# A two-block transformer kernel: the second block's projections, in another order on ScalarE and VectorE, and the compressed scores in another order on TensorE

## The chip, the cores and the metric

The kernel runs on one core of a Trainium2 chip. The metric is the device time of one execution in microseconds. A core has TensorE (PE, matmuls; PEld in the profile is its weight loads), VectorE (DVE), ScalarE (ACT), GpSimd (POOL) and SyncE (SP, here the engine that issues the weights' transfers). They run side by side, each in its own program order, and wait for each other through semaphores.

## The reference

One sequence of 256 rows, width 1024, in float32, goes through two blocks. The first is a recurrent mixer with cross attention and a mixture of experts. The second, which the change touches, begins with one projection of the normalised rows that is cut into twelve parts, and a sparse attention over three kinds of keys, one of them compressed blocks of 32 rows:

```python
xn = rmsnorm(x, norm_mix)
(u_rnn, u_gate, q, k_c, v_c, k_s, v_s, k_w, v_w, g_nsa, g_a, g_b) = jnp.split(xn @ w_in, cuts, axis=-1)
...
qh = rmsnorm(q.reshape(B, T, N_HEADS, hd), q_norm) * (hd ** -0.5)
kc = rmsnorm(compress_blocks(kv(k_c), phi_k_pe, phi_k_w1, phi_k_w2), kc_norm)
...
# compress_blocks: 15 overlapping blocks of 32 rows, each with pe added, flattened, then
#   gelu(flat @ w1) @ w2
s_c = einsum("bgrqd,bgcd->bgrqc", qb, kc) + bias          # 16 heads, 256 rows, 15 blocks
p_c = masked_softmax(s_c, cend[None, :] <= tq[:, None])
```

x there is the first block's output after its own final norm; heads have 64 elements, 16 query heads share 4 groups of keys.

## The kernel before

Every product of a projection is done three times, as high x high, high x low and low x high halves of float32 values (lines 433 to 435, `mm3`), so each weight unit has to be split before TensorE can use it. The weights come as units of 128 x 2048 values (1 MB; those of ug 128 x 1792) in a fixed plan: kcvc 0 and 1, ksvs 0 and 1, kwvw 0 and 1, q2a 0 and 1, q2b 0 and 1, ug 0 and 1, w1 0 to 3, ug 2 to 5, then the units of the attention loop. A unit passes four stations:

- SP issues its transfer into one of four slots of a ring, when TensorE has used the unit that lay there, four places earlier (line 2563).
- ACT copies it to one of three buffers for high halves (`high`, L1175). It waits for the landing, and until TensorE has used the unit three places earlier.
- DVE writes the low half over the slot (`low`, L1731).
- TensorE waits for that (s_w_lo), multiplies, and sets the unit free (s_w_used).

On ACT and DVE both steps are written by hand between their other work as `ahead(key)`, which stands for the unit two places behind key. So `ahead(("ksvs", 0))` prepares kwvw 0, and `ahead(("ug", 0))` prepares w1 0. Nothing else sets the order: it is the order in the code.

In the second block's projections TensorE does the transposes of rows (turn 4 and turn 5, L443, and the row of scales, L453), kcvc, ksvs, the bias row (L883), kwvw, q2a, q2b, the gates (gn), ug 0 and 1, w1 0 to 3, ug 2, small transposes and products (L918 to L932), the queries' and keys' transposes (L951 and L958 among them), ug 3 and 4, the compressed scores (L973), ug 5, and the attention loop, whose scores are L999 and L1002. A unit of ksvs, kwvw or q2 is 24 matmuls of 512 columns; one of w1 is 24 of 256 columns with 60-column weights, one of ug 48 of 256 columns.

DVE and ACT do around this: `blocks(p)` (L2208, 16 small additions that build the overlapping blocks), whose result ACT copies to its high half (`block_high`, L1439) and DVE completes (L1740 with 960 elements); turn 5, that is `normalise(5)` on DVE (L1760, L1740) with `turn_high(5)` on ACT (L1193); four products of the residual rows with their scale (L2222); the bias row (L2229); reading out the projections' banks (L1463, L1464, L1467 on ACT); and the norms of the heads: squares on ACT (L1475), sums on DVE (L2232), the root on ACT (L1477), the products on DVE (L2238 and L2240, for each of the two row tiles).

The compressed scores are 64 matmuls with a weight of 64 rows (one head's elements) by 128 (rows of the sequence) and 15 columns. Even heads lie on partitions 0 to 63, odd heads on 64 to 127, and `head(h)` gives which. Each of the two kinds goes into a bank of its own.

## Time and profile before

| | us |
|---|---|
| median of 3 runs | 1296.73 (1295.91 to 1301.46) |
| the profiled execution | 1296.88 |
| its span | 1295.1 |
| PE, PEld busy | 1224.7 (95%), 1085.5 (84%) |
| DVE, ACT, POOL busy | 909.2 (70%), 722.9 (56%), 116.8 (9%) |
| mean granted clock of TensorE | 0.975 |
| second block's projections | about 728 to 866 in the span |

The 1.8 us beside the span lie before the first and after the last instruction that is recorded. Busy shares are means over stages with different limits, so the stage of the change has to be read by itself, by windows and by the timelines of its engines. A matmul's recorded duration is longer than its distance to the next, because they overlap; the distance is what it costs.

### The profile page before, as it was taken

To read this page: it belongs to the slowest core of one execution; us is meant where nothing else is said; L and a number is where in the kernel's file an instruction comes from. 1 tells how busy PE (TensorE), PEld (TensorE's weight loads), DVE (VectorE), ACT (ScalarE), POOL (GpSimd) and SP (SyncE) were. 2 spreads that over 40 slices of the span, in tenths; PEclk is the share of its full clock that TensorE was granted. 3 is DMA by queue.
4 is the path that set the end of the run, shared out by engine and by line. 5 is a ranking of instruction groups with operands and counts; after the bars stand their busy time and mean duration, and the time that the engine had idled before them with its cause. 6 is when DMAs were issued, how large, how long until landed. Compare 5 with 4: busy or idle time off the path is not lost. (4 is left out here: it accounts for less than half of the span.)

```text
span 1295.1 us, 18840 instructions
## 1 busy us (share of the span) xinstructions
PE 1224.7 (95%) x7850; PEld 1085.5 (84%) x7850; DVE 909.2 (70%) x967; ACT 722.9 (56%) x838; POOL 116.8 (9%) x135
## 2 busy tenths in 40 slices
PE   6999998988999999999998889999989999899998
PEld 6988996977888787887876868898989998799997
DVE  5997587447778888788888864558755975655553
ACT  4744324444577676766766345558768734444442
POOL 0100000000000000000000100009721520000000
PEclk8999999989999999999999889889999999899999
DMA  6433325315489888888987236422225446355552
GB/s 260 162 130 131 131 98 183 131 65 195 178 324 366 317 329 325 322 340 308 365 322 283 74 131 222 172 90 98 95 82 167 153 135 212 114 195 195 195 195 98
DMA packets 38179, 255.43 MB, mean 197 GB/s; under 512 B 4192, under 2 KB 6368, under 8 KB 10320
## 3 DMA queue, kind: packets, MB, share of 16 engines
q1 hardware_dynamic: 34800, 247.64, 53.2%
q10 hardware_dynamic: 3296, 6.61, 1.4%
q8 instruction: 62, 1.02, 0.3%
q14 instruction: 21, 0.17, 0.0%
HBM read 253.15 MB, written 1.08 MB: 196 GB/s over the span
## 5 line engine op out<-in xcount | busy, mean ns | idle before, releaser
L433 PE MATMUL bank<-r,r 128*128 128x512 f32 (+5 forms) x2016 | 672.3, 333 | 44.1 <-DVE r L1731 22.1
L1731 DVE TENSOR_TENSOR r<-f,r 128x2048 fp32r<-128x2048 f32 (+3 forms) x240 | 542.8, 2267 | 202.1 <-ACT r L1175 201.9
L435 PE MATMUL bank<-r,r 128*128 128x512 f32 (+5 forms) x2016 | 661.6, 328 | 0.0
L434 PE MATMUL bank<-r,r 128*128 128x512 f32 (+5 forms) x2016 | 661.3, 328 | 0.0
L1175 ACT ACTIVATE r<-f 128x2048 fp32r<-128x2048 f32 (+3 forms) x240 | 453.6, 1891 | 185.3 <-PE bank L435 168.6
L433 PEld LDWEIGHTS bank<-r,r 128*128 128x128 f32 (+4 forms) x2016 | 379.2, 188 | 90.5 <-issue 36.3
L434 PEld LDWEIGHTS bank<-r,r 128*128 128x128 f32 (+4 forms) x2016 | 379.5, 188 | 35.2 <-issue 1.0
L435 PEld LDWEIGHTS bank<-r,r 128*128 128x128 f32 (+4 forms) x2016 | 379.5, 188 | 34.8
L1740 DVE TENSOR_TENSOR r<-f,r 128x512 fp32r<-128x512 f32 (+3 forms) x70 | 54.9, 788 | 32.1 <-ACT r L1698 11.2
L2506 POOL TENSOR_SCALAR f<-f,f 128x128 f32<-128x128 f32 (+1 forms) x64 | 64.2, 1023 | 47.1 <-DVE f L2301 47.1
L443 PE MATMUL bank<-f,f 128*128 128x128 f32 x224 | 33.2, 310 | 9.0 <-DMA f<-in_cst 6.2
L443 PEld LDWEIGHTS bank<-f,f 128*128 128x128 f32 x224 | 31.5, 222 | 11.0 <-DMA f<-in_cst 6.2
L2470 POOL TENSOR_SCALAR f<-f 128x1 f32<-128x1 f32 x2 | 0.6, 292 | 416.4 <-ACT f L1186 416.4
L1193 ACT ACTIVATE r<-f 128x512 fp32r<-128x512 f32 x28 | 17.4, 631 | 30.3 <-DVE f L1760 30.3
L1696 ACT ACTIVATE f<-bank 128x512 f32<-128x512 f32 x16 | 9.6, 600 | 41.4 <-PE bank L435 41.4
L2457 POOL TENSOR_SCALAR f<-f 128x1 f32<-128x1 f32 x10 | 4.8, 480 | 307.1 <-ACT f L1186 306.9
L1186 ACT ACTIVATE f<-f 128x512 f32<-128x512 f32 x28 | 17.5, 625 | 22.1 <-DVE f L1802 9.8
L1747 DVE TENSOR_TENSOR f<-bank,f 128x512 f32<-128x512 f32 x28 | 18.7, 687 | 15.7 <-PE bank L443 15.6
L1564 ACT ACTIVATE f<-f,f 128x128 f32<-128x128 f32 (+1 forms) x64 | 28.3, 446 | 1.9 <-DVE f L2338 1.9
L1200 ACT ACTIVATE f<-bank 128x512 f32<-128x512 f32 x12 | 7.1, 593 | 27.4 <-PE bank L435 27.3
L2423 DVE TENSOR_TENSOR f<-f 128x512 f32<-128x512 f32 x16 | 11.1, 692 | 14.7 <-ACT f L1696 14.7
L1760 DVE TENSOR_TENSOR f<-f,bank 128x512 f32<-128x512 f32 x28 | 18.5, 682 | 3.2 <-PE bank L453 3.2
(314 smaller groups left out, 998.3 us busy)
## 6 DMA issues: line engine op xcount, KB each, us to landing
f<-in_weights SPq DMA_DIRECT2D x216, 1024.0 KB, 4.9
f<-in_weights SPq DMA_DIRECT2D x12, 896.0 KB, 4.7
f<-in_weights SPq DMA_DIRECT2D x8, 672.0 KB, 4.7
f<-in_weights SPq DMA_DIRECT2D x4, 882.0 KB, 5.3
f<-bias_table ACTq DMA_DIRECT2D x1, 2048.0 KB, 13.1
f<-in_mem ACTq DMA_DIRECT2D x1, 1024.0 KB, 4.8
out<-f ACTq DMA_DIRECT2D x2, 512.0 KB, 2.6
f<-in_moe ACTq DMA_DIRECT2D x1, 647.0 KB, 3.6
```

The costliest lines, as they stand in the source:

```text
L433: e.matmul(o, lh.r, rh.r, start=start, stop=False)
L434: e.matmul(o, lh.r, rl.r, start=False, stop=False)
L435: return e.matmul(o, ll.r, rh.r, start=False, stop=stop)
L443: m = e.matmul(banks[b][:, j * 128:(j + 1) * 128], src[:, i, (4 * hf + j) * 128:(4 * hf + j + 1) * 128], C("rev") if back else ident, star ...
L1175: e.activation(high_of(n).r, slot_of(n).f, ACT.Copy).then_inc(s["w_hi"], 1)
L1186: e.activation(junk[number % 2], src[:, i, hf * 512:(hf + 1) * 512], ACT.Square, scale=1.0 / 32, accum_out=rows[r][i][2 * n + hf]).then_in ...
L1564: m = e.activation(P, P, ACT.Exp, bias=an[:, a:a + 1], accum_out=asum[:, a:a + 1])
L1731: e.tensor_tensor(slot_of(n).r, slot_of(n).f, high_of(n).r.bitcast(F32), ALU.subtract).then_inc(s["w_lo"], 1)
L1740: return e.tensor_tensor(value.r, value.f, value_high.r.bitcast(F32), ALU.subtract)
L1747: e.tensor_tensor(dst[tile_cut(hf, 1 - i if back else i)].f, banks[bank_at["turn", q, a]][:, :].rearrange("p (j t) -> p j t", j=4), gain_o ...
L1760: e.tensor_tensor(dst[pair(p)].f, dst[pair(p)].f, banks[bank_at["row", q]][:, 0:256].unsqueeze(1).to_broadcast([128, 2, 256]), ALU.mult).t ...
L2506: m = e.tensor_scalar(P, P, ari[:, a:a + 1], None, ALU.mult)
```

## The change

It has two parts. On ACT and DVE, the weights' steps are written in other places: kwvw's units are split before and between the work for the blocks, and blocks(1) now stands behind turn 5; the four products of the residual rows with their scale stand behind two more units; w1's first unit is split before the gates' copy and the squares on ACT and before the heads' sums on DVE, w1's second before the root on ACT and before the heads' products on DVE, and w1's third on DVE between the two row tiles' products. No step of computation is added or taken away. On TensorE, the compressed scores of even and odd heads alternate; both banks are taken at the start, and both are handed on at the end.

```diff
--- before.py
+++ after.py
@@ -962,18 +962,18 @@
                 proj_t("ug", 4, c, 8, 112, XTT, "ev_a")
 
 
+            bc = [take(("cs", odd)) for odd in range(2)]
+            e.wait_ge(s["qt"], 4)
+            e.wait_ge(s["kct"], 1)
+            for i in range(2):
+                for h in range(16):
+                    lo, pr, g = head(h)
+                    m = e.matmul(banks[bc[h % 2]][:, (8 * i + pr) * 15:(8 * i + pr + 1) * 15], QT[lo:lo + 64, pr, i * 128:(i + 1) * 128],
+                                 KCT[lo:lo + 64, g, :], start=True, stop=True)
+                    if i == 1 and h >= 14:
+                        full["cs", h - 14] = done(m)
             for odd in range(2):
-                b = take(("cs", odd))
-                if odd == 0:
-                    e.wait_ge(s["qt"], 4)
-                    e.wait_ge(s["kct"], 1)
-                for i in range(2):
-                    for h in range(odd, 16, 2):
-                        lo, pr, g = head(h)
-                        m = e.matmul(banks[b][:, (8 * i + pr) * 15:(8 * i + pr + 1) * 15], QT[lo:lo + 64, pr, i * 128:(i + 1) * 128],
-                                     KCT[lo:lo + 64, g, :], start=True, stop=True)
-                full["cs", odd] = done(m)
-                freed[b] = ("cs_ev", odd + 1)
+                freed[bc[odd]] = ("cs_ev", odd + 1)
             for c in range(2):
                 proj_t("ug", 5, c, 8, 112, XTT, "ev_a")
             for gh in range(2):
@@ -1439,13 +1439,16 @@
                 e.activation(BLH[:, 960 * p:960 * p + 960].r, BLP[:, 960 * p:960 * p + 960].f, ACT.Copy).then_inc(s["bl_h"], 1)
 
             ahead(("kcvc", 0))
+            ahead(("kcvc", 1))
             block_high(0)
-            ahead(("kcvc", 1))
+            ahead(("ksvs", 0))
+            turn_high(5)
+            ahead(("ksvs", 1))
             block_high(1)
-            turn_high(5)
             for name in ("ksvs", "kwvw", "q2a", "q2b"):
-                ahead((name, 0))
-                ahead((name, 1))
+                if name != "ksvs":
+                    ahead((name, 0))
+                    ahead((name, 1))
                 if name == "kwvw":
                     e.wait_ge(s["bi_t"], 1)
                     e.dma_start(table.ap(), PCC[0:16, 1024:1536]).then_inc(s["l_t"], 16)
@@ -1466,6 +1469,7 @@
                         j = int(name == "q2b")
                         m = e.activation(QKv[:, i, 8 * j:8 * j + 8, :], o.rearrange("p (g d) -> p g d", g=8), ACT.Copy)
                     read_out((name, i), m)
+            ahead(("ug", 0))
             e.wait_ge(s["pe_done"], full["gn"])
             e.activation(GNT[0:48, :], banks[bank_at["gn"]][0:48, 0:256], ACT.Copy).then_inc(s["gn_c"], 1)
             e.wait_ge(s["ev_a"], READ_AT["q2b", 1])
@@ -1473,6 +1477,7 @@
                 if i == 1:
                     e.wait_ge(s["hr_r"], 1)
                 e.activation(sqv[:, 0:1536], QK[:, i * 1536:(i + 1) * 1536], ACT.Square).then_inc(s["hr_q"], 1)
+            ahead(("ug", 1))
             e.wait_ge(s["hr_v"], 1)
             e.activation(hr, hr, ACT.Sqrt).then_inc(s["hr"], 1)
 
@@ -1480,9 +1485,7 @@
                 wait_unit(("ug", j))
                 read_out(("ug", j), e.activation(GE.f[pair(j)], banks[bank_at["ug", j]][0:112, :].rearrange("p (j t) -> p j t", j=2), ACT.Gelu_apprx_tanh))
 
-            ahead(("ug", 0))
             gelu_out(0)
-            ahead(("ug", 1))
             gelu_out(1)
             for p in range(2):
                 ahead(("w1", 2 * p))
@@ -2207,42 +2210,50 @@
                             i8 = slice(8 * half, 8 * half + 8)
                             m = e.tensor_tensor(dst[:, i8, :], w[:, 1 - par:16:2, :], pe_[hi:hi + 64, p, i8].unsqueeze(2).to_broadcast([64, 8, 15]), ALU.add)
                 read_out(("kcvc", p), m)
+
+            def block_low(p):
                 e.wait_ge(s["bl_h"], p + 1)
                 low_of(BLP[:, 960 * p:960 * p + 960], BLH[:, 960 * p:960 * p + 960]).then_inc(s["bl"], 1)
 
             ahead(("kcvc", 0))
             blocks(0)
             ahead(("kcvc", 1))
+            block_low(0)
+            ahead(("ksvs", 0))
+            normalise(5)
+            ahead(("ksvs", 1))
             blocks(1)
-            normalise(5)
-            e.wait_ge(s["n_rs"], SCALES[4] + 4)
-            for a in range(4):
-                cols = (slice(None), a // 2, slice((a % 2) * 512, (a % 2 + 1) * 512))
-                e.wait_ge(s["xf"], a + 1)
-                e.tensor_scalar(X[cols], XF[cols], rows[4][a // 2][4], None, ALU.mult).then_inc(s["x4"], 1)
-            for name in ("ksvs", "kwvw", "q2a", "q2b"):
+            block_low(1)
+            e.wait_ge(s["l_b"], 16)
+            e.wait_ge(s["pe_done"], full["bi"])
+            e.tensor_tensor(PCC[0:16, 1024:1536], banks[bank_at["bi"]][0:16, :], PCC[0:16, 512:1024], ALU.add).then_inc(s["bi_t"], 1)
+            for name in ("kwvw", "q2a", "q2b"):
                 ahead((name, 0))
                 ahead((name, 1))
-                if name == "ksvs":
-                    e.wait_ge(s["l_b"], 16)
-                    e.wait_ge(s["pe_done"], full["bi"])
-                    e.tensor_tensor(PCC[0:16, 1024:1536], banks[bank_at["bi"]][0:16, :], PCC[0:16, 512:1024], ALU.add).then_inc(s["bi_t"], 1)
+                if name == "kwvw":
+                    e.wait_ge(s["n_rs"], SCALES[4] + 4)
+                    for a in range(4):
+                        cols = (slice(None), a // 2, slice((a % 2) * 512, (a % 2 + 1) * 512))
+                        e.wait_ge(s["xf"], a + 1)
+                        e.tensor_scalar(X[cols], XF[cols], rows[4][a // 2][4], None, ALU.mult).then_inc(s["x4"], 1)
+            ahead(("ug", 0))
             for i in range(2):
                 e.wait_ge(s["hr_q"], i + 1)
                 e.tensor_reduce(hs[:, 24 * i:24 * i + 24], sqv[:, 0:1536].rearrange("p (h d) -> p h d", h=24), AX.X, ALU.add).then_inc(s["hr_r"], 1)
             e.wait_ge(s["hr_r"], 2)
             after(own(e.tensor_scalar(hs, hs, 1.0 / 64, EPS, ALU.mult, ALU.add)))
             e.reciprocal(hr, hs).then_inc(s["hr_v"], 1)
+            ahead(("ug", 1))
             e.wait_ge(s["hr"], 1)
             for i in range(2):
+                if i == 1:
+                    ahead(("w1", 0))
                 e.tensor_tensor(QKv[:, i, 0:16, :], QKv[:, i, 0:16, :], hr[:, 24 * i:24 * i + 16].unsqueeze(2).to_broadcast([128, 16, 64]), ALU.mult)
                 for u in range(2):
                     m = e.tensor_tensor(KDv[:, i, :, :, u, :].rearrange("p s g d -> p (s g) d"), QKv[:, i, 16:24, :],
                                         hr[:, 24 * i + 16:24 * i + 24].unsqueeze(2).to_broadcast([128, 8, 64]), ALU.mult)
                 m.then_inc(s["qn"], 1)
-            ahead(("ug", 0))
-            ahead(("ug", 1))
-            for u in range(4):
+            for u in range(1, 4):
                 ahead(("w1", u))
             ahead(("ug", 2))
             e.wait_ge(s["pe_done"], full["ht"])
```

On DVE, twelve rows from blocks(0) on, behind ksvs 0's low half (in the changed kernel a line's number is 3 higher: `low` is L1734, the blocks L2211). r_50 is a weight slot, f_238 the blocks, f_61 the turned rows, f_59 the residual rows. Before:

```order
L2208 TENSOR_TENSOR f_238<-bank,f_55 64x8x15 x16
L1740 TENSOR_TENSOR r_239<-f_238,r_211 128x960
L1731 TENSOR_TENSOR r_50<-f_49,r_52 128x2048
L2208 TENSOR_TENSOR f_238<-bank,f_55 64x8x15 x16
L1740 TENSOR_TENSOR r_239<-f_238,r_211 128x960
L1760 TENSOR_TENSOR f_61<-f_61,bank 128x512 x2
L1740 TENSOR_TENSOR r_62<-f_61,r_64 128x512
L1760 TENSOR_TENSOR f_61<-f_61,bank 128x512
L1740 TENSOR_TENSOR r_62<-f_61,r_64 128x512
L1760 TENSOR_TENSOR f_61<-f_61,bank 128x512
L1740 TENSOR_TENSOR r_62<-f_61,r_64 128x512 x2
L2222 TENSOR_SCALAR f_59<-f_131,f_67 128x512 x4
```

After:

```order
L2211 TENSOR_TENSOR f_238<-bank,f_55 64x8x15 x16
L1734 TENSOR_TENSOR r_50<-f_49,r_52 128x2048
L1743 TENSOR_TENSOR r_239<-f_238,r_211 128x960
L1734 TENSOR_TENSOR r_50<-f_49,r_52 128x2048
L1763 TENSOR_TENSOR f_61<-f_61,bank 128x512 x2
L1743 TENSOR_TENSOR r_62<-f_61,r_64 128x512
L1763 TENSOR_TENSOR f_61<-f_61,bank 128x512
L1743 TENSOR_TENSOR r_62<-f_61,r_64 128x512
L1763 TENSOR_TENSOR f_61<-f_61,bank 128x512
L1743 TENSOR_TENSOR r_62<-f_61,r_64 128x512 x2
L1734 TENSOR_TENSOR r_50<-f_49,r_52 128x2048
L2211 TENSOR_TENSOR f_238<-bank,f_55 64x8x15 x16
```

ksvs 1's and kwvw 0's low halves stand now ahead of turn 5 and kwvw 1's behind it, all three ahead of blocks(1); before, only ksvs 1's stood in this stretch, and kwvw's two came behind blocks(1), turn 5 and the products.

On DVE, around the heads' norms (f_67 holds sums and scales, f_232 the heads). Before:

```order
L1731 TENSOR_TENSOR r_50<-f_49,r_52 128x1792 x2
L2232 TENSOR_REDUCE f_67<-f_220 128x24 x2
L2234 TENSOR_SCALAR f_67<-f_67 128x48
L2235 RECIPROCAL f_67<-f_67 128x48
L2238 TENSOR_TENSOR f_232<-f_232,f_67 128x1024
L2240 TENSOR_TENSOR f_208<-f_232,f_67 128x8x64 x2
L2238 TENSOR_TENSOR f_232<-f_232,f_67 128x1024
L2240 TENSOR_TENSOR f_208<-f_232,f_67 128x8x64 x2
L1731 TENSOR_TENSOR r_50<-f_49,r_52 128x2048 x4
L1731 TENSOR_TENSOR r_50<-f_49,r_52 128x1792 x3
```

After:

```order
L1734 TENSOR_TENSOR r_50<-f_49,r_52 128x1792 x2
L1734 TENSOR_TENSOR r_50<-f_49,r_52 128x2048
L2242 TENSOR_REDUCE f_67<-f_220 128x24 x2
L2244 TENSOR_SCALAR f_67<-f_67 128x48
L2245 RECIPROCAL f_67<-f_67 128x48
L1734 TENSOR_TENSOR r_50<-f_49,r_52 128x2048
L2251 TENSOR_TENSOR f_232<-f_232,f_67 128x1024
L2253 TENSOR_TENSOR f_208<-f_232,f_67 128x8x64 x2
L1734 TENSOR_TENSOR r_50<-f_49,r_52 128x2048
L2251 TENSOR_TENSOR f_232<-f_232,f_67 128x1024
L2253 TENSOR_TENSOR f_208<-f_232,f_67 128x8x64 x2
L1734 TENSOR_TENSOR r_50<-f_49,r_52 128x2048
```

One low half of w1 stands now ahead of the sums, one ahead of the products and one between them; before, four came behind them all.

On PE, the compressed scores with bank numbers and waits, ahead of them the end of ug 4. Before:

```order
L435 MATMUL bank3<-r8_64,r1_50 112x256
L973 MATMUL bank4<-f102_252,f88_224 128x15 [waits s_kct,s_qt]
L973 MATMUL bank4<-f102_252,f88_224 128x15 x15
L973 MATMUL bank5<-f102_252,f88_224 128x15 [waits s_ev_a]
L973 MATMUL bank5<-f102_252,f88_224 128x15 x15
L433 MATMUL bank6<-r8_64,r2_52 112x256 [waits s_w_lo,s_kt]
```

After:

```order
L435 MATMUL bank3<-r8_64,r1_50 112x256
L971 MATMUL bank4<-f102_252,f88_224 128x15 [waits s_qt,s_kct,s_ev_a]
L971 MATMUL bank5<-f102_252,f88_224 128x15
L971 MATMUL bank4<-f102_252,f88_224 128x15
L971 MATMUL bank5<-f102_252,f88_224 128x15
L971 MATMUL bank4<-f102_252,f88_224 128x15
```

The pairs of rows with bank4 and bank5 go on so to the 64th matmul. What was two lists, one for each bank, is one that changes the bank with every matmul; the wait for the second bank's reader (s_ev_a) stands now at the first.

## Rows read from the trace of the kernel before

**Rows 1.** Windows, all engines: length, busy us (instructions), PE clock, DMA.

```profile
739.65:751.00 11.35, 11.35 (x51) 8.88 (x49) 9.38 (x22) 3.12 (x4) 0.00 (x0) 1.00 0.51 185
752.05:758.20 6.15, 0.01 (x2) 0.01 (x1) 6.05 (x10) 5.58 (x9) 0.22 (x1) 0.85 0.47 171
758.20:763.20 5.00, 5.00 (x12) 3.94 (x13) 4.92 (x3) 1.92 (x2) 0.00 (x0) 0.50 0.00 0
808.20:812.05 3.85, 0.00 (x0) 0.01 (x1) 3.85 (x5) 3.85 (x4) 0.00 (x0) 0.86 0.74 251
812.05:817.65 5.60, 5.58 (x27) 5.60 (x28) 4.28 (x2) 0.81 (x2) 0.00 (x0) 0.50 0.04 15
817.65:825.80 8.15, 8.15 (x71) 8.15 (x70) 4.11 (x2) 4.14 (x4) 0.00 (x0) 0.99 0.81 278
850.20:858.50 8.30, 8.30 (x65) 8.26 (x65) 0.41 (x1) 1.88 (x2) 0.00 (x0) 0.81 0.35 126
858.50:862.05 3.55, 3.55 (x17) 3.55 (x17) 2.67 (x5) 1.62 (x2) 0.00 (x0) 0.50 0.00 0
866.00:961.00 95.00, 91.13 (x888) 82.51 (x886) 72.51 (x142) 74.06 (x204) 64.24 (x64) 1.00 0.30 100
```

**Rows 2.** Timeline, PE: start, us, line, operation [idle before, its releaser].

```profile
758.19 0.79 PE L433 MATMUL bank<-r,r 128*128 128x512 f32 x1 [6.14 <-DVE r L1731]
812.08 0.44 PE L433 MATMUL bank<-r,r 128*60 128x256 f32 x1 [3.90 <-DVE r L1731]
```

**Rows 3.** Timeline, ACT, around the first hole.

```profile
746.86 1.01 ACT L1439 ACTIVATE r<-f 128x960 fp32r<-128x960 f32 x1 [6.29 <-DVE f L2208]
753.53 3.69 ACT L1175 ACTIVATE r<-f 128x2048 fp32r<-128x2048 f32 x2
757.13 0.36 ACT L1463 ACTIVATE f<-bank 128x256 f32<-128x256 f32 x1
```

**Rows 4.** Timeline, DVE, around the first hole.

```profile
742.93 3.90 DVE L2208 TENSOR_TENSOR f<-bank,f 64x120 f32<-64x120 f32 x16
747.89 1.16 DVE L1740 TENSOR_TENSOR r<-f,r 128x960 fp32r<-128x960 f32 x1 [1.07 <-ACT r L1439]
749.09 1.28 DVE L1760 TENSOR_TENSOR f<-f,bank 128x512 f32<-128x512 f32 x2
754.27 1.67 DVE L2222 TENSOR_SCALAR f<-f,f 128x512 f32<-128x512 f32 x4
```

**Rows 5.** Timeline, ACT and DVE, ahead of the second hole.

```profile
790.83 1.70 ACT L1175 ACTIVATE r<-f 128x1792 fp32r<-128x1792 f32 x1 [5.51 <-DMA f<-in_weights]
...
807.30 1.22 DVE L2238 TENSOR_TENSOR f<-f,f 128x1024 f32<-128x1024 f32 x1
809.64 2.29 DVE L1731 TENSOR_TENSOR r<-f,r 128x2048 fp32r<-128x2048 f32 x1
```

**Rows 6.** SP's transfers from 728 on; PE behind kcvc; the page's DMA row.

```profile
733.83 132.51 SPq L2563 DMA_DIRECT2D f<-in_weights  x20
...
739.29 0.60 PE L453 MATMUL bank<-f,f 128*128 128x128 f32 x4
...
f<-in_weights SPq DMA_DIRECT2D x216, 1024.0 KB, 4.9
```

**Rows 7.** L999's line (ns min/median/max), then timeline, PE: runs of small matmuls.

```profile
L999 PE MATMUL bank<-f,f x64: 272/272/373, 866.8 to 937.8; 64*128 64x128 f32 x64
...
833.01 1.95 PE L932 MATMUL bank<-f,f 128*15 128x64 f32 x32 [0.48 <-DVE f L2249]
842.26 1.91 PE L951 MATMUL bank<-f,f 128*128 128x128 f32 x16
850.20 2.96 PE L973 MATMUL bank<-f,f 64*128 64x15 f32 x25
866.78 0.71 PE L999 MATMUL bank<-f,f 64*128 64x128 f32 x8
```

**Rows 8.** Timeline, DVE: the last product of the compressed softmax.

```profile
862.66 0.66 DVE L2289 TENSOR_TENSOR f<-f,f 128x480 f32<-128x480 f32 x1
```

## The prediction

> **What bounds the kernel now.** I read the page first: TensorE (PE) is busy for 95% of the span, VectorE (DVE) 70%, ScalarE (ACT) 56%, and the chain that ended last is mostly PE. So a microsecond is won only where PE stands still, runs at half clock, or does its work less densely. The stage windows of the second block's projections [rows 1] show three such places. PE is empty from 752.05 to 758.20 (6.15 us) and then works 5.00 us at a granted clock of 0.50; it is empty again from 808.20 to 812.05 (3.85 us) and works 5.60 us at 0.50; and the compressed scores take 8.30 us from 850.20 to 858.50 at a mean of 0.81, after which the clock stays at 0.50 (1.2 GHz of its two levels 1.2 and 2.4) until 862.05. In the stretch behind, 866 to 961, the clock is 1.00 and PE has 91.1 of 95 us busy, so what is gained before it reaches the end.
>
> Both holes end on the same releaser: the low half of a weight unit by DVE [rows 2]. Why it is late stands in the engines' own order. First hole: ACT makes the high halves of kwvw at 753.53, behind block_high(1) and the four high halves of turn 5 [rows 3]; DVE makes the low half behind blocks(1) (742.93), its low half, turn 5 (from 749.09) and the four L2222 products (from 754.27) [rows 4]. PE had asked for it at 752.05. Second hole: the low half of w1's first unit starts on DVE at 809.64, behind the sums, the reciprocal and the products of the heads' norms, the last of them from 807.30 [rows 5]; on ACT the high half stands behind the squares and the root.
>
> **First hole.** The weights' chain is now ahead of the blocks. From rows: the high half of ksvs1 needs kcvc0 used (733.8, when the next transfer is issued [rows 6]), so it is done at 735.7 (two in 3.69 us, 1.9 each, [rows 3]); blocks(0) on DVE ends at 737.7, ksvs1's low half (2.3 us, [rows 5]) at 740.0, and PE wants it at 745.3. block_low(0) ends at 741.2. kwvw0's high half needs kcvc1 used at 739.3 (PE's L453 follows it) and its landing, 733.8 + 4.9 [rows 6] = 738.7: ACT 739.3 to 741.2, DVE to 743.5, against PE's 752.05. Turn 5 (5.2 us with ACT's share between, from 749.09 to 754.27, [rows 4]) runs from 743.5 to 748.7. kwvw1: ACT 748.0 to 749.9, DVE to 752.1; PE wants it at 757.7. Now blocks(1) (3.9 us) runs to 756.0, ACT's high to 757.0, DVE's low (1.16) to 758.2, the table row behind it. ACT empties the ksvs banks (four of 0.36 that overlap, [rows 3], 1.1 us) and makes q2a0's high half at 758.1 to 760.0, DVE's low half ends at 762.3; PE, without the hole, has done kwvw's two units (the two units of ksvs, 48 matmuls, took 11.35 us, [rows 1]) at 763.4. So the hole is gone whole, with about 1 us to spare at the next unit; the one after (q2a1) is ready at 764.5 against 769.1, and the four L2222 products (1.7 us) lie in that spare time. The hole's worth is 6.15 us. The half clock followed the empty stretch, so it goes with it: 12 matmuls in 5.00 us, at the full pace of 11.35/48 = 0.236 us they take 2.8, which gives 2.2 us.
>
> **Second hole.** PE's work from 758.20 to 808.20 is then 50.0 - 2.2 = 47.8 us long and starts at 752.05: it comes to w1 at 799.9. w1's first unit: ACT's high half stands now before gn's copy and the squares, DVE's low half before the sums. Its slot was released by q2b0 at about 780.3. Landings are 4.9 us, and 7.7 at worst behind the 2 MB bias load (q2a's second unit ends at 758.2 + 2.2 + 4 x 5.65 = 783.0 before; the high half of the unit that follows into its slot waited for the transfer until 790.8, [rows 5]), so landed at 788.0 at the latest; ACT needs 1.9 and DVE 2.3: 792.2, against 799.9. Second unit: its high half needs ug0 used (48 x 0.115 = 5.5 before 799.9, 794.4), ACT to 796.3, DVE to 798.6, in place of the heads' products. The hole of 3.85 us goes, and its half clock: 27 matmuls in 5.60 us, at 8.15/71 = 0.115 us each 3.1, gives 2.5 us.
>
> **What is late next.** w1's units are short: 24 x 0.115 = 2.8 us, so four are 11.1 us, while a slot needs landing 4.9 + ACT 1.9 + DVE 2.3 = 9.1 us from its release. w1's fourth unit takes ug1's slot, released at 799.9: landed 804.8. DVE before it: w1's third (ACT waits for ug1, empties it, 800.5 to 802.4; DVE to 804.7), then the second row tile's head products (807.30 to 809.64, 2.3 us, [rows 5]) to 807.0, then the fourth's low half to 809.3. PE wants it at 808.3: a new hole of 1.0 us. ug2 (slot of w1's first, released at 802.7) is ready at 811.8 against 812.1. From below this hole is 0, from above, with a landing of 7.7 us instead of 4.9 in this and the following two units, 3.8 us. I take 1.0.
>
> **Compressed scores.** 64 matmuls of a 64x128 weight and 15 columns, now even and odd heads in turn, rows 0 to 63 and 64 to 127 of the array, each into its own bank. A run's row lasts to the end of its last matmul, which is recorded with 0.27 us (L999's, [rows 7]; I take it for all of these). The first 25 before stand (2.96 - 0.27)/24 = 0.112 us apart at full clock, as far apart as L951's with 128 rows and 128 columns ((1.91 - 0.27)/15 = 0.109): the pace is that of loading a weight, not of the 15 columns. L999 in this kernel already alternates the two row ranges with weights of 64x128 and 128 columns: 8 of them in 0.71 us, (0.71 - 0.27)/7 = 0.063 apart [rows 7]. So 64 x 0.063 = 4.0; the densest small matmuls here, L932, stand (1.95 - 0.27)/31 = 0.054 apart, 3.5 us. Upper bound: no pairing, 64 x 0.112 = 7.2, or 8.3 as it is with its half clock. I take 3.8, near L999: gain 4.5, bounds 0 and 4.8. A mean of 0.81 over 8.3 us means that the last 2 x 0.19 x 8.3 = 3.2 us were at half clock, so it fell 5.1 us into that stretch, and a stretch of 3.8 us between dense work more likely ends before it. Then ug5's first 17 matmuls take 17 x 0.115 = 1.95 instead of 3.55: 1.6 us. Behind it, the softmax chain on DVE took from 858.61 to 863.3 [rows 8]; it now starts both bank reads after the end (0.4 more) and needs 5.0 us, ug5 at full clock covers 5.5, so PE's L984 does not wait.
>
> The Trainium skill has a rule that speaks against this part. "TensorEngine Tiling (Array Packing)", under Performance Considerations, Instruction Overhead, says that each matmul carries about 60 cycles of overhead and that a tiling factor should not be taken out of a dimension that is already small. By it 15 columns would not profit, and the sum would be that of the second rival. The trace agrees only so far: 15 columns cost as much as 128, but the pace seen is that of the weight, whose rows are halved here, and L999's pairs show it shared.
>
> **Sum.** 6.15 + 2.2 + 3.85 + 2.5 - 1.0 + 4.5 + 1.6 = 19.8 us. The profiled execution took 1296.88 us with a span of 1295.1; its time is the median of the runs (1296.73) within 0.2. 1296.9 - 19.8 = 1277.1 us.
>
> **Rivals.**
> - Clock still falls at the scores. What speaks for it: the fall before came while they ran, and small matmuls follow small ones. Against: the stretch is less than half as long. Where it falls, some 6.8 us (the 3.2 and 3.55 of [rows 1]) run at half speed again and 3.4 us come back: 1280.5.
> - The row ranges don't overlap at 15 columns (the change doesn't do what it says there): 7.2 us for the scores and the clock as before: the last two terms shrink from 6.1 to about 0.5: 1282.7. L999 is against it.
> - w1 and the units behind it starve: a hole of 3.8 us instead of 1.0 and, since the clock fell 4.3 and 2.8 us into the two holes (their means of 0.85 and 0.86, [rows 1]), half clock behind it (2.5): 1282.4. For it: the 9.1 us of the slot's way against 8.4 us of matmuls. Against: only one unit falls short by the rows.
> - Only moved: the blocks' late work makes q2a0 late by as much as kwvw was. ACT waits in block_high(1) for blocks(1) with q2a0's high half queued behind it. It has 1 us of slack; each microsecond of DVE beyond it costs one. With 6 us late, and the half clock, the first two terms (8.35) go: 1285.5.
> - Slower: the denser feed has PE reach the attention loop (866 to 961 before) with its lists of small matmuls at a low clock and stay there. There the clock is 1.00 now with 91.1 us busy; at 0.50 through the whole loop it would cost up to 45 us: 1322. It decides only if the clock falls for more than 2 x 19.8 = 40 us of it. Nothing in the rows speaks for it: the loop's work is the same and was reached out of a clock of 1.00 before.
>
> **Chances.** The forecast 0.60; clock at the scores 0.14; no overlap 0.05; w1 starves 0.10; only moved 0.05, within 0.5% (several of these at once, 1290 and above) 0.04; slower 0.02. What a measurement of this kernel can tell from no change is about 0.5%, 6.5 us. So faster 0.94, same 0.04, slower 0.02. The range goes from 1272.5, where the new hole is absent and the later dips of the clock fall 3 us more kindly, to 1284, which takes in the clock, overlap and w1 cases.
>
> **What would show it.** PE's wait on L1734 (L1731 before) at the start of kwvw and at the start of w1 gone, PEclk 1.00 through both; a short wait at w1's fourth unit; L971's 64 matmuls in about 4 us with starts in pairs; ug5 all at full clock; L984 not waiting. The prediction is wrong if a hole of over 2 us stands at q2a0 or w1, if L971 takes 7 us, or if the 866 to 961 stretch (now some 20 us earlier) is longer than 95 us.

## The result, and the profile after

| us | before | after |
|---|---|---|
| median | 1297.2 (1295.6 to 1301.5, 6 runs) | 1283.66 (1279.62 to 1287.07, 6 runs) |
| the profiled execution | 1296.88 | 1287.07 |
| its span | 1295.1 | 1285.3 |

The ratio is 0.988 (0.9859 to 0.9902): 13.5 us faster, where 19.8 were forecast; 1283.7 lies at the upper end of the range. The profiled execution of the changed kernel is the slowest of its six, 3.4 us over their median, so its own gain is only 9.8.

The windows of the changed kernel that answer to [rows 1], all engines (length, busy us and instructions of PE, PEld, DVE, ACT and POOL, PE clock, DMA share, GB/s):

```profile
752.00:763.20 11.20, 11.20 (x47) 8.39 (x46) 8.98 (x20) 6.04 (x9) 0.00 (x0) 1.00 0.52 190
763.20:785.70 22.50, 22.50 (x100) 18.46 (x99) 11.20 (x10) 9.56 (x10) 0.22 (x1) 1.00 0.78 267
836.50:840.50 4.00, 4.00 (x65) 3.97 (x64) 0.00 (x0) 1.88 (x2) 0.00 (x0) 0.91 0.69 238
840.50:846.60 6.10, 6.10 (x30) 6.06 (x31) 5.00 (x10) 3.47 (x3) 0.00 (x0) 0.50 0.04 16
1020.60:1024.70 4.10, 0.12 (x2) 0.03 (x1) 4.10 (x5) 2.22 (x2) 2.31 (x2) 0.92 0.59 166
1024.70:1031.00 6.30, 6.29 (x30) 6.30 (x31) 6.30 (x6) 2.22 (x2) 1.54 (x1) 0.51 0.00 1
```

The first two rows are kwvw and q2a: no hole, and the clock at 1.00. The third is the compressed scores, in 4.00 us instead of 8.30. The fourth is ug5 at half clock all through. The last two lie far behind the change, at the fourth unit of pb, and are dealt with below. (pb is the projection of the attention's result, `y_b @ proj_b`, in four units of weights behind the attention loop; pa is `y_a @ proj_a`, the one behind it.)

PE's waits for a weight's low half between 740 and 1060 in the changed kernel (us in total, times, longest), then the two rows of its timeline that answer to [rows 2]:

```profile
PE bank L433 <- DVE r L1734: 7.1, 3, 4.0
```

```profile
809.70 0.33 PE L433 MATMUL bank<-r,r 128*60 128x256 f32 x1 [1.13 <-DVE r L1734]
...
1024.70 0.55 PE L433 MATMUL bank<-r,r 128*128 128x256 f32 x1 [3.98 <-DVE r L1734]
```

Both large waits of [rows 2], 6.14 and 3.90, are gone. A wait of 1.13 us stands at w1's fourth unit, where 1.0 was forecast. The wait of 3.98 is not new, but it was 2.37 in the kernel before. The third of the three, 1.96 us at 998.17, was 1.95 before.

How far the changed kernel runs ahead is best read from the start of one and the same matmul in each trace, minus its start in the kernel before. The columns are times in the trace of before; every number is worked out from two rows of PE's timeline. The kernels below the first two lines are the experiments.

| us | 745 | 768 | 806 | 831 | 868 | 1004 | 1035 | 1052 | 1130 | 1280 |
|---|---|---|---|---|---|---|---|---|---|---|
| after | +0.8 | -7.6 | -8.0 | -13.7 | -16.9 | -16.6 | -18.2 | -13.8 | -12.7 | -9.8 |
| after_again | -0.2 | -8.6 | -9.1 | -14.9 | -18.0 | -17.9 | -19.5 | -15.3 | -14.7 | -14.7 |
| scores_only | +0.2 | +0.2 | -0.1 | +0.2 | -4.2 | -4.0 | -5.4 | -1.3 | -0.6 | -0.6 |
| order_only | -0.3 | -8.7 | -9.1 | -14.8 | -11.5 | -11.0 | -12.6 | -8.3 | -7.7 | -7.7 |
| blocks_only | +0.1 | -8.4 | -8.8 | -9.7 | -8.1 | -8.0 | -9.6 | -6.7 | -6.3 | -5.8 |
| heads_only | -1.5 | -1.5 | -1.8 | -7.7 | -6.1 | -5.8 | -7.4 | -3.1 | -2.4 | -2.4 |
| scores_in_ug4 | +0.5 | -8.0 | -8.4 | -14.3 | -18.9 | -20.3 | -21.9 | -17.7 | -17.1 | -17.1 |
| pb3_earlier | +0.1 | -8.4 | -8.8 | -14.7 | -17.9 | -17.8 | -19.4 | -19.5 | -19.9 | -19.9 |
| all_three | -0.3 | -8.7 | -9.2 | -15.0 | -19.7 | -21.1 | -21.1 | -22.9 | -23.6 | -23.6 |
| before_pb3 | -0.1 | -0.1 | -0.1 | -0.2 | -0.3 | -0.2 | -0.2 | -2.0 | -1.1 | -1.1 |

The first line shows where the gain arises and where it is lost. Against its lead ahead of the change (+0.8), the first hole gives 8.8 us (forecast 8.35), the second 5.7 (3.85 + 2.5 - 1.0 = 5.35 forecast), the scores with ug5 3.2 (6.1 forecast): 17.7 us in the stages that the change touches. The attention loop leaves that as it is. Then the lead falls from 18.2 to 13.8 at one wait, and creeps down by another 4 us to the end.

### The profile page after: what moved, and what is told of

Same layout as the page of the kernel before. It is cut to its first block and busy times, and to the rows that moved or that the text cites. A ratio compares the mean times of both kernels' runs of the same rounds, so it can differ in the third digit from the quotient of the medians.

```text
span 1285.3 us, 18841 instructions
## 1 busy us (share of the span) xinstructions
PE 1222.2 (95%) x7850; PEld 1084.2 (84%) x7850; DVE 909.5 (71%) x967; ACT 722.6 (56%) x838; POOL 116.3 (9%) x135
## 5 line engine op out<-in xcount | busy, mean ns | idle before, releaser
L433 PE MATMUL bank<-r,r 128*128 128x512 f32 (+5 forms) x2016 | 673.9, 334 | 36.9 <-DVE r L1734 15.3
L1734 DVE TENSOR_TENSOR r<-f,r 128x2048 fp32r<-128x2048 f32 (+3 forms) x240 | 542.8, 2267 | 195.2 <-ACT r L1175 194.6
L2434 DVE TENSOR_TENSOR f<-f 128x512 f32<-128x512 f32 x16 | 11.1, 692 | 18.2 <-ACT f L1699 18.2
## 6 DMA issues: line engine op xcount, KB each, us to landing
f<-bias_table ACTq DMA_DIRECT2D x1, 2048.0 KB, 13.5
```

The source lines that it names most:

```text
L433: e.matmul(o, lh.r, rh.r, start=start, stop=False)
L1734: e.tensor_tensor(slot_of(n).r, slot_of(n).f, high_of(n).r.bitcast(F32), ALU.subtract).then_inc(s["w_lo"], 1)
```

## Experiments

Six of them ask where the gain arises, five where it went. "Before" ran beside each: 1298.09, 1297.75 and 1297.93 in the three groups that were timed, 17 or 18 runs each. Ratios are against it, with their 95% intervals.

### The parts of the change

**scores_only** is the kernel before with the alternated scores alone:

```diff
+            bc = [take(("cs", odd)) for odd in range(2)]
...
+            for i in range(2):
+                for h in range(16):
+                    lo, pr, g = head(h)
+                    m = e.matmul(banks[bc[h % 2]][...
...
-                    for h in range(odd, 16, 2):
```

> The kernel before with only the compressed scores' order changed: even and odd heads alternate. Theory A (the pairs of row ranges are what shortens this part, and the half clock behind it still falls, as in the changed kernel's trace): the 64 matmuls take 3.7 to 4.1 us instead of 8.3, some 3 to 6.5 us less in all, 1291 to 1294; with half clock over the scores' end and ug5 the lower gain, without it the upper. Rival B (the pairs save nothing at 15 columns): within 1 us of the kernel before. Both holes of 6.1 and 3.9 us stay where they were.

Measured: 1295.03, ratio 0.9972 (0.9956 to 0.9988). The windows of its scores and of what follows:

```profile
850.00:853.80 3.80, 3.80 (x64) 3.66 (x62) 0.04 (x1) 1.88 (x2) 0.00 (x0) 1.00 0.48 157
853.80:859.00 5.20, 5.20 (x40) 5.17 (x39) 3.53 (x9) 2.25 (x3) 0.00 (x0) 0.67 0.21 87
```

The scores take 3.8 us as forecast, and here the clock falls only behind them. The stage gives 4.4 us (+0.2 to -4.2). Between 1035 and 1052 the lead falls by 4.1, and 0.8 are left at the end of this trace; in the medians it is 3.1. The time lies 1 us above theory A's range and 3 below the kernel before, so rival B, that the pairs save nothing, did not happen.

**order_only** is the changed kernel with the scores in their old order (the diff above, the other way round).

> The changed kernel with the compressed scores in the old order: only the order on ACT and DVE differs from the kernel before. Theory A (the parts add): 13.5 to 14.5 us less by the end of w1 and ug2, and 8.3 us for the scores with their half clock; the time 11 to 14 below before, 1283 to 1286. Rival B (what is won at the holes is given back later at the wait for pb's last unit, 4.4 us in the changed kernel's trace, whenever PE comes early): only 9 to 10 below, 1287 to 1288, with a wait of 4 us and half clock at pb's fourth unit in the trace.

Measured: 1287.62, ratio 0.9916 (0.9894 to 0.9939): 10.5 us. With scores_only's 3.1 that makes 13.6, against 14.35 of the whole (after_again) beside the same "before": within their intervals, which are some us wide, the two parts add. The time itself is the one that rival B named (1287 to 1288), and so are the wait of 3.99 us at pb's fourth unit, at 1030.31, and the lead's fall there from 12.6 to 8.3. The scores took theory A's 8.3 us; what it left out is ug5 behind them. Its windows of the scores (two rows) and ug5 show what the old order costs behind the new one:

```profile
833.00:838.20 5.20, 5.20 (x48) 5.06 (x46) 1.80 (x3) 1.88 (x2) 0.00 (x0) 1.00 0.30 88
838.20:841.30 3.10, 3.10 (x21) 3.10 (x20) 0.41 (x1) 0.00 (x0) 0.00 (x0) 0.51 0.47 196
841.30:848.00 6.70, 6.70 (x32) 6.66 (x32) 1.72 (x3) 0.11 (x1) 0.00 (x0) 0.50 0.00 0
```

ug5 stays at half clock for 6.70 us, where it was 3.55 before [rows 1], and the lead shrinks from 14.8 to 11.5 there. The clock fell 5.2 us into the scores here and 5.1 in the kernel before; what differs is how long it stayed down, here to the end of ug5. So what a run of sparse matmuls costs depends also on how long half clock lasts behind it, and not on the run alone.

**after_again** is the changed kernel once more.

> The changed kernel once more, for a second trace. Theory A (the 4.4 us at pb's fourth unit and the 3 us of slower 256-column matmuls in the MLP depend on the single execution): the trace shows another pattern of half clock, and the matmuls of the MLP stand either 113 to 114 or 117 to 118 ns apart; the time 1280 to 1287 as before. Rival B (they belong to the kernel): the same wait of 4 us with half clock behind it at pb's fourth unit and 117.8 ns in the MLP again.

Measured: 1283.74, ratio 0.9888 (0.9864 to 0.9913), with a profiled execution of 1282.2 instead of 1287.07. The wait at pb's fourth unit is there again, 3.99 us, with half clock behind it: that part belongs to the kernel. In the table it agrees with the first trace to 0.3 us up to 1035, once the 1.0 us that it leads at 745 is taken off; from 1130 on it keeps its 14.7, where the first trace slid from 12.7 to 9.8. The reason stands in two rows of each trace, five matmuls apart in the same stage. After:

```profile
1229.81 0.28 PE L435 MATMUL bank<-r,r 128*128 128x256 f32 x1
...
1230.40 0.28 PE L434 MATMUL bank<-r,r 128*128 128x256 f32 x1
```

The same kernel again:

```profile
1229.74 0.28 PE L435 MATMUL bank<-r,r 128*128 128x256 f32 x1
...
1230.31 0.28 PE L434 MATMUL bank<-r,r 128*128 128x256 f32 x1
```

0.59 against 0.57 us for five: 118 ns from start to start instead of 114, over the last stage some 3 us. It belongs to the one execution, at the same granted clock. Of all the traces only the first of the changed kernel has it through the whole last stage, and blocks_only for some 20 us of it (from 1115 in its own time, where five matmuls take 0.59 us too). The second trace of the changed kernel lacks it, so it is no part of what the change does; why it comes was not found.

**blocks_only** is the kernel before with the first part of the reordering, the weights ahead of the blocks:

```diff
             ahead(("kcvc", 1))
-            blocks(1)
+            block_low(0)
+            ahead(("ksvs", 0))
             normalise(5)
...
+            ahead(("ksvs", 1))
+            blocks(1)
+            block_low(1)
```

> The kernel before with only the order around the blocks changed (kwvw's units split before blocks(1), the residual products later), heads and scores as before. Theory A (each hole is worth itself and the half clock behind it): no hole at kwvw, 8.9 us less by the end of q2b as in the changed kernel's trace, the hole of 3.9 us at w1 still there; the time 8 to 9 below before. Rival B (the hole only moves: with PE earlier, the hole at w1 grows by what was won, since w1's split hangs on the heads' chain): less than 5 below.

**heads_only** is the kernel before with the second part, w1's first units ahead of the heads' norms:

```diff
+            ahead(("ug", 0))
             for i in range(2):
                 e.wait_ge(s["hr_q"], i + 1)
...
+            ahead(("ug", 1))
             e.wait_ge(s["hr"], 1)
             for i in range(2):
+                if i == 1:
+                    ahead(("w1", 0))
```

> The kernel before with only w1's first three units split earlier, around the heads' sums and products. Theory A: the hole of 3.9 us at w1 and 5.6 us of half clock go, a hole of about 1 us at w1's fourth unit comes, 5 to 6 us less; the hole of 6.1 us at kwvw stays. Rival B (w1's split only looked late and the landing of its slots bounds it): a hole of 3 us at w1's fourth unit or at ug2 and 2 to 3 us less in all.

Measured: blocks_only 1289.99, ratio 0.9940 (0.9918 to 0.9963); heads_only 1294.03, ratio 0.9963 (0.9942 to 0.9983). Each removes its own hole and leaves the other. PE's timeline of heads_only, then of blocks_only:

```profile
756.73 0.80 PE L433 MATMUL bank<-r,r 128*128 128x512 f32 x1 [6.16 <-DVE r L1731]
```

```profile
803.30 0.30 PE L433 MATMUL bank<-r,r 128*60 128x256 f32 x1 [3.90 <-DVE r L1734]
```

8.9 us (+0.1 to -8.8) and 5.9 (-1.8 to -7.7) are won on the spot, as theory A of each had it; heads_only has the new wait at w1's fourth unit too, 0.92 us. At the end of the traces 5.9 and 0.9 of them are left, from 745, so each part alone loses in the later stages too. The medians, 7.8 and 3.7 below before, keep more than these two single traces.

### The clock at the scores

The scores run at the pace that was forecast, and still the clock fell. L971's line in the changed kernel (ns min, median, max; first and last start), for [rows 7]:

```profile
L971 PE MATMUL bank<-f,f x64: 258/258/370, 836.5 to 840.3; 64*128 64x15 f32 x64
```

The 64 recorded passes, which stood as 64 matmuls above, are 32 matmuls in the code (16 heads, two row tiles), each of float32 values and recorded twice; the starts come in pairs 7 ns apart, with 105 ns to the next pair, 0.056 us for each pass. From 839.8 on they and ug5 run at half clock. **scores_in_ug4** keeps the alternation and spreads the scores in four groups of 8 matmuls over ug4's:

```diff
+            def some_scores(n):
+                for k in range(8 * n, 8 * n + 8):
+                    i, h = k // 16, k % 16
...
+            for c in range(2):
+                proj_t("ug", 4, c, 8, 112, XTT, "ev_a", among=lambda k: some_scores(k // 4 + 2 * c) if k % 4 == 3 else None)
```

> The changed kernel with the 32 score matmuls in four groups of 8 between the matmuls of ug 4, instead of one stretch between ug 4 and ug 5. Theory A (the clock falls because the scores are one stretch of sparse work): no half clock between ug 4 and the attention loop, 3 us less than the changed kernel, near 1280. Rival B (it falls from something else there): the half clock stays near ug 5 and the time is that of the changed kernel.

Measured: 1278.63, ratio 0.9844 (0.9816 to 0.9873), 5.1 us below after_again beside it. One of its four groups on PE's timeline, and its windows through ug4 with all the scores and through ug5:

```profile
832.15 1.07 PE L972 MATMUL bank<-f,f 64*128 64x15 f32 x16
```

```profile
829.00:838.80 9.80, 9.12 (x98) 8.37 (x97) 3.83 (x5) 3.71 (x5) 0.00 (x0) 1.00 0.29 95
838.80:844.50 5.70, 5.70 (x57) 5.53 (x56) 2.43 (x5) 2.91 (x4) 0.00 (x0) 1.00 0.33 96
```

(1.07 - 0.26)/15 = 0.054 us for each pass, the same work and the same pace, but the clock stays at 1.00 in both windows. Counted from 745, the lead is 1.6 us more than after_again's at 868 (a new wait of 0.68 us takes a part: ug4 now begins only when DVE has read out the keys, which the scores among it need), and 3.1 more at 1004 and at the end; the other 1.5 us come around 945 in these kernels' own time (961 in the kernel before, which has it as well), where the changed kernel runs 3.4 us at half clock and this one doesn't:

```profile
830.94 0.34 PE L433 MATMUL bank<-r,r 128*112 128x256 f32 x1 [0.68 <-DVE f L2282]
```

```profile
941.00:950.00 9.00, 7.45 (x77) 6.98 (x78) 4.21 (x3) 5.46 (x8) 0.00 (x0) 1.00 0.24 79
```

So the traces show 3.1 us and the medians 5.1. The rival "clock still falls at the scores" is what happened. The clock fell where the small matmuls stood together and not where the same number stood in four groups, in this trace and in those of all_three and all_four below. The half clock around 945 is another matter: all_four has the scores spread too, and there it is back:

```profile
943.30:946.70 3.40, 3.40 (x18) 3.40 (x17) 1.96 (x1) 1.41 (x1) 0.00 (x0) 0.50 0.06 17
```

So only the 1.6 us at the scores are shown to be the spreading's; why the later 1.5 came isn't shown.

### Where the lead is lost

After the attention loop, PE waits at pb's fourth unit for the low half, in all traces without an edit there. Rows of DVE, and of PE at its end, before:

```profile
1031.87 3.46 DVE L2360 TENSOR_TENSOR_SCAN f<-f,f 112x256 f32<-112x256 f32 x3 [1.74 <-POOL f L2521]
...
1035.83 3.13 DVE L2360 TENSOR_TENSOR_SCAN f<-f,f 112x256 f32<-112x256 f32 x3
1038.88 2.26 DVE L1731 TENSOR_TENSOR r<-f,r 128x2048 fp32r<-128x2048 f32 x1
```

```profile
1041.29 0.36 PE L433 MATMUL bank<-r,r 128*128 128x256 f32 x1 [2.37 <-DVE r L1731]
```

After, DVE (PE's row, 1024.70, stands above):

```profile
1015.27 3.46 DVE L2371 TENSOR_TENSOR_SCAN f<-f,f 112x256 f32<-112x256 f32 x3 [1.75 <-POOL f L2532]
1018.66 0.65 DVE L2381 SCALAR_TENSOR_TENSOR f<-f,bank 128x512 f32<-128x512 f32 x1
1019.24 3.14 DVE L2371 TENSOR_TENSOR_SCAN f<-f,f 112x256 f32<-112x256 f32 x3
1022.30 2.26 DVE L1734 TENSOR_TENSOR r<-f,r 128x2048 fp32r<-128x2048 f32 x1
```

The weight's low half stands behind two runs of three scans (the recurrent branch's, on DVE), and the first run starts when POOL is done. That chain follows by 16.6 us (1031.87 to 1015.27), as PE does at 1004. PE itself is by then 18.2 ahead, since the kernel before runs 3.4 us at half clock around 1016 and the changed one does not. So PE comes 1.6 us more ahead than the chain, and waits 3.98 instead of 2.37. This does not grow with the lead: between 1035 and 1052 it falls by 4.1 us in scores_only, which is 5.4 ahead, by 4.3 in order_only, 12.6 ahead, and by 4.4 in the changed kernel, 18.2 ahead. And behind the longer wait the clock is down: 0.51 over 6.30 us in the last row of the first fence. In the kernel before it was 1.00 in the same place:

```profile
1041.30:1047.60 6.30, 6.30 (x53) 6.30 (x54) 6.30 (x6) 2.54 (x3) 1.55 (x1) 1.00 0.17 50
```

**pb3_earlier** takes the low half in front of the second run of scans, which don't need it; nothing else is changed:

```diff
             lru_scan(2)
+            ahead(("pb", 1))
             gated_b(0)
             lru_scan(3)
-            ahead(("pb", 1))
             lru_low(2)
```

> The changed kernel with the low half of pb's fourth unit on DVE moved ahead of gated_b(0) and the second scan, which waits for POOL. Theory A (the wait of 4 us at pb's fourth unit and the half clock behind it are made by that low half standing behind the scan): the wait goes, a shorter one stands at pa's first unit, 3 to 5 us less than the changed kernel. Rival B (the chain of POOL and the scans bounds PE there, and the wait only moves to pa): the wait appears at pa's first unit in its full length, within 1 us of the changed kernel.

Measured: 1276.94, ratio 0.9840 (0.9818 to 0.9861), 6.8 us below the changed kernel (1283.74) where 3 to 5 were expected. Its rows on DVE and PE and its windows:

```profile
1014.12 3.46 DVE L2371 TENSOR_TENSOR_SCAN f<-f,f 112x256 f32<-112x256 f32 x3 [1.76 <-POOL f L2532]
1017.49 2.27 DVE L1734 TENSOR_TENSOR r<-f,r 128x2048 fp32r<-128x2048 f32 x1
```

```profile
1019.90 0.36 PE L433 MATMUL bank<-r,r 128*128 128x256 f32 x1 [0.36 <-DVE r L1734]
```

```profile
1020.00:1026.00 6.00, 5.80 (x48) 5.59 (x48) 6.00 (x7) 2.46 (x3) 3.94 (x2) 1.00 0.38 115
```

The wait is 0.36, the clock stays up, and the lead of 19.4 us at 1035 is still 19.9 at the end. Counted from 745, that is 5.5 us more than after_again's: 3.6 of the wait and 3.4 of the half clock, less 1.65 that PE now stands in front of pa's first unit:

```profile
1027.45 0.36 PE L433 MATMUL bank<-r,r 112*128 112x256 f32 x1 [1.65 <-issue]
```

**all_three** joins both edits to the changed kernel: the scores spread through ug4, and the low half earlier.

> The changed kernel with the scores among ug 4's matmuls and the low half of pb's fourth unit earlier on DVE. Theory A (both are independent): 1278.6 less 3 to 5, that is 1274 to 1276. Rival B (what is won at one is lost at the other): near 1278.

Measured: 1275.24, ratio 0.9826 (0.9800 to 0.9851), the best median of all: 22.5 us below before, 8.4 below the changed kernel. It is 1.7 us below pb3_earlier, where the spreading of the scores gave 5.1 without the pb edit; between the two traces it is 3.3 (23.3 against 20.0, from 745). The ranges of the runs overlap (1273.29 to 1280.03 against 1276.55 to 1280.09), and 1.5 of the 3.3 us arise around 945, where pb3_earlier has half clock and all_three has none. So whether the edits add in full stays open.

**before_pb3** makes the same edit of pb in the kernel before.

> The kernel before with the low half of pb's fourth unit earlier on DVE, as pb3_earlier has it on the changed kernel, where it took 6.8 us off. Theory A (part of what the change won is given back at this wait: it is 2.4 us without half clock behind it in both traces of the kernel before, 4.0 with 6.8 us of half clock in the changed kernel): here the same edit brings only 1 to 3 us, 1295 to 1297. Rival B (the wait costs both kernels the same and the change gave nothing back there): 6 to 7 us here too, 1291 to 1292.

Measured: 1296.61, ratio 0.9992 (0.9978 to 1.0005). There the edit is worth 1.3 us, which can't be told from nothing, but is clear of rival B's 6 to 7. The same edit is worth 6.8 us behind the change. So behind the change this wait costs 5.5 us more in the medians (6.8 less 1.3) than it did before, and 4.5 in the traces (5.5 less 1.0).

**before_again** is the kernel before once more, to see whether its shorter wait was an accident of the one profile.

> The kernel before once more, for a second trace. Theory A (its first trace, on which the prediction stands, caught a mild execution at pb's fourth unit: a half clock of 3.4 us just ahead of it held PE back, so the wait was 2.4 us and no half clock followed): now a wait near 4 us with half clock behind it, as in every kernel traced since, and the span from the end of the scores' stage on 3 to 4 us longer. Rival B (only the changed order makes PE come early there): a wait of 2.4 us and no half clock behind it again.

Measured: 1299.44 in one run. PE's row and the window behind it:

```profile
1043.88 0.36 PE L433 MATMUL bank<-r,r 128*128 128x256 f32 x1 [2.37 <-DVE r L1731]
```

```profile
1043.70:1050.00 6.30, 6.12 (x52) 6.15 (x53) 6.30 (x7) 2.35 (x3) 1.74 (x1) 1.00 0.17 54
```

2.37 again, and full clock behind it. So the mild case belongs to the kernel before, and theory A of this run fell. Its 3.4 us at half clock ahead of the wait, around 1016, is there in the three traces of kernels that have none of the change (before, before_again, before_pb3), and in none of the eight of kernels with a part of it or all of it (with the scores spread alone too). But it is back in all_three, 994.90 to 998.30 at 0.50, and in all_four. Why the clock falls there in the ones and not in the others was not settled: the work in that stretch is the same, and so is PE's wait of 1.95 to 1.97 us at its start.

### The new wait at w1's fourth unit

**all_four** is all_three with w1's fourth low half ahead of the second row tile's head products:

```diff
                     ahead(("w1", 0))
+                    ahead(("w1", 1))
...
-            for u in range(1, 4):
+            for u in range(2, 4):
                 ahead(("w1", u))
```

> The kernel all_three with the low half of w1's fourth unit ahead of the second row tile's head products. Theory A (the wait of 1.1 us at w1's fourth unit is DVE's order, as the prediction had it): the wait shrinks to 0.5 or less. Rival B (its landing sets it: the high half starts on the landing in the traces): the wait stays within 0.3 us of 1.1. The time 1275, within 1 us of all_three, either way.

Measured: 1276.36, ratio 0.9836 (0.9818 to 0.9853), not to be told from all_three. The rows of ACT and PE in all_three, then in all_four:

```profile
803.83 1.92 ACT L1180 ACTIVATE r<-f 128x2048 fp32r<-128x2048 f32 x1 [2.37 <-DMA f<-in_weights]
...
808.38 0.33 PE L433 MATMUL bank<-r,r 128*60 128x256 f32 x1 [0.92 <-DVE r L1739]
```

```profile
803.55 1.92 ACT L1180 ACTIVATE r<-f 128x2048 fp32r<-128x2048 f32 x1 [2.54 <-DMA f<-in_weights]
...
807.85 0.34 PE L433 MATMUL bank<-r,r 128*60 128x256 f32 x1 [0.84 <-DVE r L1739]
```

The wait stays (0.92, then 0.84), and rival B came: ACT's high half waits 2.4 to 2.5 us for the landing in both, and in all_four DVE stands idle for 2.16 us before the low half until ACT is done. The forecast's own reason, DVE's products, holds in the changed kernel all the same. Its rows of ACT and DVE:

```profile
804.96 1.92 ACT L1175 ACTIVATE r<-f 128x2048 fp32r<-128x2048 f32 x1 [2.17 <-DMA f<-in_weights]
```

```profile
806.16 1.29 DVE L2253 TENSOR_TENSOR f<-f,f 128x512 f32<-128x512 f32 x2
807.37 4.22 DVE L1734 TENSOR_TENSOR r<-f,r 128x2048 fp32r<-128x2048 f32 x2
```

The high half is done at 806.88, the products at 807.45, and the low half follows them without a gap. So the products end last, but only by about half a microsecond; take them away, and the transfer stands in nearly the same place. Moving them has a price as well: DVE idles for the landing with the products still to do, so ug2's low half starts at 810.05 instead of about 808.2 (all_three), and PE has a new wait for it:

```profile
812.21 0.34 PE L433 MATMUL bank<-r,r 128*112 128x256 f32 x1 [1.36 <-DVE r L1739]
```

## Why the prediction was right in direction and too large

- **First hole: right.** 8.35 forecast, 8.8 measured, 8.8 and 8.9 in order_only and blocks_only. The tight place that it named held as well. The rows of DVE in the changed kernel:

```profile
753.25 3.88 DVE L2211 TENSOR_TENSOR f<-bank,f 64x120 f32<-64x120 f32 x16
758.21 1.16 DVE L1743 TENSOR_TENSOR r<-f,r 128x960 fp32r<-128x960 f32 x1 [1.08 <-ACT r L1439]
...
761.10 4.49 DVE L1734 TENSOR_TENSOR r<-f,r 128x2048 fp32r<-128x2048 f32 x2 [1.02 <-ACT r L1175]
```

  q2a's first low half is done at 763.35 (4.49 for two), and PE, 0.8 us behind before's time here, wants it at about 764.2: 0.9 us to spare, where about 1 was forecast. "Only moved" did not happen.
- **Second hole: right.** 5.35 net forecast, 5.7 measured, the new wait 1.13 for 1.0. The rival of a wait of 3.8 us did not happen. The reason given for the 1.0 holds by the rows, with the transfer half a microsecond behind it (all_four).
- **Pace of the scores: right.** 3.8 us forecast, 3.8 to 4.0 measured; the row ranges do overlap at 15 columns. The prediction read the Trainium skill's rule ("TensorEngine Tiling (Array Packing)", Instruction Overhead) as speaking against it. That rule is about the dimension that the tiling factor is taken out of, and here this is the 64 rows of a head and not the 15 columns, so it doesn't speak against the pairs; the measurement decides in any case. In this kernel, where each of these matmuls loads its own weight, alternating halved the distance from 0.112 to 0.056.
- **Clock at the scores: the first step that failed.** "A stretch of 3.8 us between dense work more likely ends before it": the clock fell 3.3 us into the stretch, and the scores with ug5 gave 3.2 of 6.1 us. The half-clock stretch had been tied to the place where it fell before (5.1 us in), as if that were a constant. The rival had put 3.4 us on it; 2.9 were missing, and spreading the scores (scores_in_ug4) brought 1.6 back on the spot, 3.1 by the whole trace and 5.1 by the medians. The recorded busy share gave no warning: it reads 4.00 of 4.00 us there. The Trainium skill ("TensorE: Matmul & The Clock Gate", Part 1) says that the gate goes by how busy TensorE has been recently; read by the recorded busy time, this trace does not agree, since the clock fell in a stretch that is recorded as busy throughout.
- **"What is gained before it reaches the end": the second step that failed.** It was argued from the attention loop's windows and from those alone, and there it holds (16.9 at 868, 16.6 at 1004). It was not checked for the stages behind. At pb's fourth unit the low half hangs on POOL's chain through two runs of scans, and the row of it (2.37 us) could be read in the trace of before. In the kernel before, a half-clock stretch ahead of that wait held PE back by 1.6 us; in the eight traces with a part of the change or all of it that stretch was absent, PE came 1.6 us sooner than the chain, and behind the longer wait the clock was down. Moving that one low half (pb3_earlier) took the wait and the half clock away. No rival had it.
- **The sum.** In after_again's trace: 17.8 us in the changed stages, 0.1 lost in the loop, 2.6 net from 1004 to 1052 (1.6 gained ahead of the wait, 4.2 lost at and behind it), 0.6 at 1118, where a half-clock stretch of 6.9 us ends that both traces have and that lasts to about 1 us later in after_again, by the same matmul: 14.5 at the end, and 14.35 between the medians. Of the 5.3 us that this lacks against 19.8, 2.0 are those of the scores less what the holes gave above the forecast, and 3.3 lie behind the attention loop. The first trace lacks 3 more, by its matmuls' spacing.

## What to carry to other kernels

A gain that is read at a hole counts only up to the next place where the engine waits for a chain of its own time. List the later waits of the same engine with their releasers before writing that it reaches the end, and move what stands in front of the late ones. A run of small matmuls is cheaper both in alternate row ranges and spread among dense ones; the second kept the clock there, and the first alone did not. An edit that is worth 1 us before another change can be worth 7 behind it, so such edits are to be tried again after every gain.

## What was not expected of the hardware

- Pairs of matmuls on rows 0 to 63 and 64 to 127, with 15 columns and a weight for each, start 7 ns apart with 105 ns to the next pair (L971 in the changed kernel); without alternation they stand 112 ns apart ([rows 7]).
- The clock fell 3.3 us into a stretch of such matmuls in the changed kernel, 5.1 and 5.2 in the old order (before, order_only), and behind a stretch of 3.8 us in scores_only. Spread as 4 groups of 1.07 us it did not fall.
- Behind pb's wait of 2.37 us the clock was at 1.00 in two traces, behind one of 3.98 at 0.51; the two traces had half clock shortly ahead of the wait, the other had not.
- Half-clock stretches came and went far from any edit: around 961 and around 1016 in the kernel before's time, 3.4 us each, with the same work and the same waits there.
- One and the same kernel ran 256-column matmuls 118 ns apart in one execution and 114 in another, at full granted clock in both, some 3 us in all.
